# A decoder trunk in fp32: the two chunks behind each norm on unnormed tokens, and a reordered opening and last norm

## The reference, cut to what matters

```python
def rmsnorm(x, g):
    y = x * lax.rsqrt(jnp.mean(x * x, axis=-1, keepdims=True) + EPS)
    return y * g

c_act = jax.nn.silu(c)
for layer in range(2):
    shift, scale, gate = jnp.split(c_act @ ada_w[layer, 0] + ada_b[layer, 0], 3, axis=-1)
    hn = rmsnorm(x, norm_g[layer, 0]) * (1.0 + scale) + shift
    y = rglru_mlstm_mixer(hn, ...) if layer == 0 else stick_breaking_mixer(hn, ...)
    x = x + gate * y
    shift, scale, gate = jnp.split(c_act @ ada_w[layer, 1] + ada_b[layer, 1], 3, axis=-1)
    hn = rmsnorm(x, norm_g[layer, 1]) * (1.0 + scale) + shift
    x = x + gate * ((silu(hn @ w1) * (hn @ w3)) @ w2)
return rmsnorm(x, final_g)
```

## Time and profile before

| | |
|---|---|
| median of 3 runs | 2367.89 us (2367.54 to 2368.1) |
| profiled execution | 2365.77 us, its span 2363.9 us |
| PE busy | 2302.2 us (97%) |
| PEld, DVE, ACT, POOL busy | 1971.4, 1771.0, 940.4, 183.2 us |
| chain that ended last | PE 91%, DMA 4%, DVE 2%, issue 1%, ACT 1% |
| DMA | 619.80 MB, mean 262 GB/s |

### The profile page before, as it was taken

The page is one execution under the profiler, slowest core; times in us unless marked ns, Lnnn a source line. Parts: engine busy times, 40 slices in busy tenths (PEclk is TensorE's granted clock), DMA queues, the critical chain, the costliest instruction groups (busy, mean ns, idle before and its releaser), DMA issues.

```text
span 2363.9 us, 35433 instructions
## 1 busy us (share of the span) xinstructions
PE 2302.2 (97%) x12570; PEld 1971.4 (83%) x12570; DVE 1771.0 (75%) x2216; ACT 940.4 (40%) x1101; POOL 183.2 (8%) x177
## 2 busy tenths in 40 slices
PE   5999999999999999999999999998999999999998
PEld 3668888788888888888878888887888888888887
DVE  6766789888878888888976656599887566656665
ACT  2011343544433443344455554435443344433442
POOL 0000005200000000000500000260000000000012
PEclk9999999999999999999999999999999999999999
DMA  9998778577777777777866666576775555555554
GB/s 381 422 409 358 292 291 311 189 302 272 294 286 268 287 284 280 281 288 283 315 230 239 265 248 231 189 291 221 291 288 220 189 193 180 194 186 189 187 205 159
DMA packets 86616, 619.80 MB, mean 262 GB/s; under 512 B 10264, under 2 KB 10520, under 8 KB 11544
## 3 DMA queue, kind: packets, MB, share of 16 engines
q1 hardware_dynamic: 85680, 617.79, 68.7%
q10 hardware_dynamic: 872, 1.15, 0.1%
HBM read 616.80 MB, written 2.10 MB: 262 GB/s over the span
## 4 chain that ended last, share of the span: by engine, by line
PE 91%; DMA 4%; DVE 2%; issue 1%; ACT 1%; SPq 0%; POOL 0%; DVEq 0%; POOLq 0%; ACTq 0%
PE ps L1125 49%; PE ps L1123 12%; PE ps L1128 12%; PE ps L1075 6%; DMA adaw<-ada_dram 4%; PE ps L1062 3%; PE ps L1039 2%; DVE adaw L686 1%; PE ps L1086 1%; PE ps L1041 1%; PE ps L1092 1%; DVE wlow L678 1%; PE ps L1270 0%; PE ps L1170 0%; PE ps L1266 0%
## 5 line engine op out<-in xcount | busy, mean ns | idle before, releaser
L497 ACT ACTIVATE whigh<-raw 128x1024 fp32r<-128x1024 f32 x704 | 732.6, 1043 | 1024.1 <-PE ps L1125 996.1
L678 DVE TENSOR_TENSOR wlow<-raw,whigh 128x1024 fp32r<-128x1024 f32 x704 | 855.4, 1219 | 282.0 <-ACT whigh L497 268.9
L1125 PE MATMUL ps<-hn,whigh 128*128 128x512 f32 x3232 | 1018.1, 396 | 0.0
L1125 PE MATMUL ps<-mid,whigh 128*128 128x512 f32 x1856 | 585.1, 396 | 1.4 <-DVE wlow L678 0.8
L1125 PEld LDWEIGHTS ps<-hn,whigh 128*128 128x128 f32 x3232 | 493.2, 189 | 0.3
L1123 PE MATMUL ps<-hn,wlow 128*128 128x256 f32 x1616 | 449.7, 278 | 0.0
L1128 PE MATMUL ps<-hn,wlow 128*128 128x256 f32 x1616 | 448.2, 277 | 0.0
L686 DVE CUSTOM_DVE_ANT_0 adaw<-adaw,cact 128x2048 f32<-128x2048 f32 x152 | 354.2, 2332 | 28.5 <-DMA adaw<-ada_dram 28.5
L1123 PEld LDWEIGHTS ps<-hn,wlow 128*128 128x128 f32 x1616 | 303.3, 188 | 73.9
L1128 PEld LDWEIGHTS ps<-hn,wlow 128*128 128x128 f32 x1616 | 303.8, 188 | 69.2
L1125 PEld LDWEIGHTS ps<-mid,whigh 128*128 128x128 f32 x1856 | 283.3, 189 | 2.7 <-issue 2.0
(11 more groups left out here) (213 smaller groups left out, 1480.5 us busy)
## 6 DMA issues: line engine op xcount, KB each, us to landing
raw<-wts_dram SPq DMA_DIRECT2D x386, 1024.0 KB, 4.8
adaw<-ada_dram SPq DMA_DIRECT2D x152, 1024.0 KB, 6.7
adaw_more<-ada_dram SPq DMA_DIRECT2D x24, 1024.0 KB, 9.8
raw<-ada_dram SPq DMA_DIRECT2D x16, 1024.0 KB, 12.1
work<-wts_dram SPq DMA_DIRECT2D x6, 1024.0 KB, 10.4
x<-xT_dram SPq DMA_DIRECT2D x4, 512.0 KB, 11.1
out_dram<-x SPq DMA_DIRECT2D x4, 512.0 KB, 2.6
cact<-c_row_dram SPq DMA_DIRECT2D x1, 1024.0 KB, 4.8
```

The lines of the kernel that those rows point to most:

```text
L497: act.activation(whigh[:, (2 * s + h) % 4, 0:width], raw[:, s, h * HALF:h * HALF + width], ACT.Copy)\
L678: dve.tensor_tensor(wlow[:, half, 0:width], raw[:, s, h * HALF:h * HALF + width], whigh[:, half, 0:width].bitcast(F32), ALU.subtract).then ...
L1125: ins = pe.matmul(ps[:, s, :], whigh[:, half, w], src[:, kk, :, :], start=kk == 0, stop=kk == kts - 1, skip_group_check=True)
```

## The change

Four things are changed.

**Raw first chunks.** In the first body behind norms 1, 2 and 3, chunks 0 and 1 are no longer split. ScalarE makes `tokens`, x times slope without the root of the variance, one tile at a time during the last body before the norm (the last tile within the norm), and puts the shift beside it as a 257th column. TensorE multiplies the float32 chunk with these 257 columns (`raw_pair`), chunk 0 and then chunk 1, and runs the norm's own small products inside chunk 0, behind its tiles 6 and 10. VectorE multiplies the finished chunk by the kept 1/root and adds the column of the shift. Tile 15 is squared by ScalarE. The normed tokens are still made, for chunks 2 and 3 and the bodies behind, now in four scalings of four tiles and 16 low parts. Chunks 0 and 1 lie in places 2 and 3 of `raw`, and chunks 2 and 3 in places 0 and 1, where they are split in the body before.

**Banks and units.** Chunks of `k` are summed in banks 2, 3, 0, 1. The first `k` body takes four units in place of two, and the last `out1` body none in place of two.

**Softplus** is computed for both pairs of heads function by function. `fresh_half` asks for three split halves at its start and for the fourth at tile 8.

**Opening and last norm.** The reciprocal is taken at tile 0, before the units of tile 1, and the mixer's constants at tile 8. TensorE runs 56 small products before its first sum of squares and 14 behind it. The quarters of squares are added in another way. In the last norm ScalarE squares tile 15, the table for the root is loaded earlier, and TensorE runs three small products ahead of the sums and one behind them.

```diff
-RSTD_STEP = 1
-CONST_STEP = 3
+CONST_STEP = 8
+TOKEN_TILES = [(range(0, 3), range(3, 6)), (range(6, 9), range(9, 12)), (range(12, 13), ()), (range(13, 15), ())]
+VARIANCE_AT, SPREAD_AT = 6, 10
...
-    body(IN1 + 1, "k", 0, 0, 73, 2)
+    body(IN1 + 1, "k", 0, 0, 73, 4)
...
-    bodies(OUT1 + 1, DOWN - 1, "out1", 85, 2, i0=1)
+    bodies(OUT1 + 1, DOWN - 2, "out1", 86, 2, i0=1)
+    body(OUT1 + DOWN - 1, "out1", 0, DOWN - 1, 0, 0, last=True)
...
+def bank(kind, s):
+    return (s + 2) % CH if kind == "k" else s
...
+def split_next(n, s, raw_start_next):
+    if raw_start_next and s >= 2:
+        return n + 1, s, True
+    return (*split_lead(n, s), False)
...
+def place_of(s, raw_start):
+    return (s + 2) % CH if raw_start else s
...
+                        if starts_raw(kind, fresh) and held < 2:
+                            sp.wait_ge(S["halves_multiplied"], n * 8 + 2 * held + 2 + CREDIT)
+                        else:
+                            sp.wait_ge(S["low_ready"], n * 8 + 2 * held + 2)
...
+            def tokens_tile(norm, m):
+                if m >= 12:
+                    act.wait_ge(S["chunks_evicted"], LAST_UPDATE[norm] * CH + m + 1 + CREDIT)
+                act.activation(tokens[:, m, 0:T], x[:, m, :], ACT.Copy, scale=slope[:, m:m + 1]).then_inc(S["tokens_ready"], 1)
...
             def norm(i):
-                act.wait_ge(S["consts_ready"], 5)
-                act.activation(warm[:, :], epsb[:, :], ACT.Sqrt)
+                act.wait_ge(S["chunks_evicted"], LAST_UPDATE[i] * CH + KT + CREDIT)
+                act.activation(last_square, x[:, KT - 1, :], ACT.Square).then_inc(S["last_squared"], 1)
...
+            def rescaled(i, dst, s):
+                dve.tensor_copy(raw_col[:, s:s + 1], ps[:, s, T:T + 1]).then_inc(S["raw_columns"], 1)
+                dve.tensor_tensor(dst, ps[:, s, 0:T], rstd_kept, ALU.mult).then_inc(S["raw_scaled"], 1)
+
+            def scaled(i, j):
+                dve.wait_ge(S["tokens_ready"], (KT + 1) * (i - 1) + 4 * j + 5)
+                if j > 1:
+                    dve.wait_ge(S["hn_ready"], KT * (i - 1) + 4 * j - 4)
+                dve.tensor_tensor(normed(j), tokens[:, 4 * j:4 * j + 4, 0:T],
+                                  rstd_kept.rearrange("p (a t) -> p a t", a=1).to_broadcast([P, 4, T]), ALU.mult)\
                    .then_inc(S["scaled_ready"], 1)
...
-                pe.wait_ge(S["low_ready"], n * 8 + 4)
+                pe.wait_ge(S["low_ready"], n * 8 + 3)
                 for kk in range(KT):
+                    if kk == HK:
+                        pe.wait_ge(S["low_ready"], n * 8 + 4)
...
+            def raw_pair(n, kind):
+                norm = NORM_OF[kind]
+                for s in range(2):
+                    pe.wait_ge(S["chunks_evicted"], n * CH + s + 1)
+                    place = place_of(s, True)
+                    pe.wait_ge(weight_loaded[place], weight_count(n, place))
+                    for k in range(KT):
+                        pe.wait_ge(S["tokens_ready"], (KT + 1) * (norm - 1) + k + 2)
+                        ins = pe.matmul(ps[:, s, 0:T + 1], raw[:, place, k * P:k * P + P], tokens[:, k, :], start=k == 0, stop=k == KT - 1,
+                                        skip_group_check=True)
+                        if s == 0 and k == VARIANCE_AT:
+                            variance(norm)
+                        elif s == 0 and k == SPREAD_AT:
+                            spread(norm)
+                    ins.then_inc(S["halves_multiplied"], 2)
...
+            def variance(c):
+                pe.wait_ge(S["square_step"], 31 * c)
+                column_sums(squares_sum, True)
+                pe.wait_ge(S["last_squared"], c)
+                column_sums(last_square, False).then_inc(S["variance_ready"], 1)
...
                     pe.wait_ge(S["consts_ready"], 5)
-                    pe.wait_ge(S["squares_added"], 3)
-                    for m in range(4):
-                        ins = pe.matmul(ps[:, 7, 0:T], ones[:, :], start_squares[:, m, :], start=m == 0, stop=m == 3)
+                    keep_busy(56)
+                    for i, m in enumerate((12, 13, 0, 1)):
+                        pe.wait_ge(S["squares_added"], 3 + i // 2)
+                        ins = pe.matmul(ps[:, 7, 0:T], ones[:, :], start_squares[:, m, :], start=i == 0, stop=i == 3)
                     ins.then_inc(S["variance_ready"], 1)
+                    keep_busy(14)
```

More of the change, by code:

```diff
@@ L142, in run_stream @@
     body(OUT0 + 2, "out0", 0, 2, 39, 2)
-    body(OUT0 + 3, "out0", 0, 3, 40, 0)
+    body(OUT0 + 3, "out0", 0, 3, 40, 0, last=True)
     between("norm", 1)
@@ L174, in second_width, with starts_raw, raw_start_next @@
     return HALF
[L177 to L187 removed]
+def place_of(s, raw_start):
+    return (s + 2) % CH if raw_start else s
+def starts_raw(kind, fresh):
+    return fresh and kind in NORM_OF
+def raw_start_next(units, last):
+    return last and units >= 0
 def bass_trunk(nc, xT, c_row, wts, ada, ada_b, norm_g, wgate, conv, lru_w, lru_b, lam, gate_b, mnorm_g, out):
@@ L372, in full_body, with body @@
                             load_unit(u + 2)
-            def body(n, kind, q, i, pair, units, fresh=False, inner={}):
+            def body(n, kind, q, i, pair, units, fresh=False, inner={}, last=False):
                 if kind in FULL:
```

264 lines of the change are left out of this document (165 added, 99 removed).

## The result

The changed kernel takes 2338.15 us (median of 4 runs, 2336.82 to 2338.48), the kernel before 2367.9 us (4 runs, 2367.54 to 2368.1): a ratio of 0.9876, 95% interval 0.9862 to 0.989, so 29.7 us or 1.2% faster. The forecast was 2341 in a range of 2335 to 2352. The profiled execution took 2336.82 us, its span is 2335.1 us, 28.8 us less than before; forecast were 27.1.

What follows compares the result with a forecast made beforehand. TensorE was taken as the bound, 91% of the chain of waits, with long pauses and low clock behind them. Terms 17.8+6.6+2.4+0.3 = 27.1 us took the profiled 2365.77 to 2338.7; with 2.1 for the median, about 2341, range 2335 to 2352.

Steps and rivals of the forecast that it cites:

- Norms (17.8 us): Norms 1 to 3: a raw pair of 15.6 us replaces stretches of 20.1, 21.8 and 22.7, gaining 17.8 us.
- VectorE behind the norm: VectorE's norm work of 13.2 us ends at 461.8, so TensorE does not pause; bad end 0.9 us at norms 1 and 3.
- `out1` (6.6): Start of `out1`: the 3.97 us pause and half of 5.30 us at low clock go, gaining 6.6 us.
- Banks of k and the four-unit body (0): Attention: new bank order and two more units in the first k body change nothing; up to 2 us if VectorE overflows.
- Opening (2.4): Opening: tile 0 starts near 25, done at 32 before the DMA queue runs dry; gain 2.4 us, bounds 0.5 to 3.
- `out0` (0): `out0` may start 1.2 us sooner, but its pair ends on the mixer's last part, which does not move: zero.
- rival B: From the softplus-and-wait run's expectation: all 1.3 us at `out0` come from the three-halves wait, giving 2360.0 us.
- Last norm (0.3): Last norm: ScalarE's square of about 0.4 us replaces GpSimd's 0.61, and small products run at full clock: 0.3 us.
- 1: Norms: VectorE falls behind, costing 3 us a norm, 9 in sum, giving 2350 us; chance 0.13.
- 2: Pauses of `out1` and the opening stay, 9 us less gain, giving 2350 us; chance 0.09.
- 3: Slower: float32 matmuls with 257 columns take twice 0.43 us, costing 41.7 us more, giving 2382 us; chance 0.04.
- Rival 4: More gain than counted, as VectorE's shorter wait for splits frees the following bodies: 2336 us; chance 0.06.

Runs made afterwards that it cites:

- e3: The kernel before, with TensorE's pauses at norms 1 to 3 filled by 19 matmuls that nobody reads: 2364.01 us, ratio 0.9989.
- e6: The changed kernel with the spread of the reciprocal root behind tile 6 of the second raw chunk instead of tile 10 of the first: 2345.6 us, ratio 0.9913.
- e1: The kernel before with only the softplus table by table and the fresh pairs of out0 and out1 waiting for three halves, not four: 2359.94 us, ratio 0.9973.
- e10: The kernel before with the pauses of norms 1 to 3 filled by matmuls and VectorE's 16 scalings at each left out: 2356.7 us, ratio 0.9956.
- e7: The changed kernel without the 56 and 14 small products that keep TensorE busy in the opening: 2336.96 us, ratio 0.9877.
- e5: The changed kernel with the spread of the reciprocal root behind tile 15 of the first raw chunk instead of tile 10: 2338.2 us, ratio 0.9882.
- e2: The kernel before with only the softplus of the scores done table by table: 2363.05 us, ratio 0.9986.

## Why the prediction was right

**Norms (17.8 us).** 19.9 measured, 19.4 less what the bodies behind take back. The steps on which the sum rests were right: no pause ahead of the pair, PEclk 1.00, the root in time, 0.434 us per raw matmul. The mis-sized term is the new stretch: I set 15.6 us, it is 14.9, since the sums took 0.81 instead of 1.0, the spread 0.44 instead of 0.7, and chunk 2 starts before the end of the last raw matmul. That is 0.7 us three times. The sum took the old stretch as one number. Beside it stood a wrong reading, that the low clock costs 2.6 us of it at norm 1: e3 brought the clock back and the pair still took 13.38 us instead of 13.65, because VectorE paced it. The reading did not enter the sum, and so did no harm. At norm 1 the closeness is also luck, since the old stretch there lay anywhere from 19.0 to 21.3 us and the prediction had one profile of it.

**VectorE behind the norm.** I put its end at 461.8 against an old start of 442.1, 19.7 us behind; it was 456.61-439.02 = 17.6. Upper values for 21 operations in a row added up to 1.8 us of false load: the last seven low parts took 2.86 us, 0.41 each, not 0.48. My bad end of 0.9 us a norm never came; by e6 the margin is 2.5 us.

**`out1` (6.6).** 6.5 measured, and e1 with only these two edits gives the same 6.5. The working also named the right reason for needing three halves only. Of the 6.6, the 2.65 for the clock are the lucky part: behind the same pause of 3.97 us e3 and e10 paid 1.5 and 1.3. The masks cost no wait.
By the Trainium skill, SBUF — State Buffer, section Who interferes with whom, the port is held for a whole instruction and the loser is blocked. Eight masks at the quiet rate of the earlier trace rows are 2.06 us; they took 3.98, so 1.9 us were lost beside the two splits of VectorE, which ran for 2.59. That agrees roughly with the rule. My 0.5 us came from using it wrongly, with one split lost for each mask where there were only two splits.

**Banks of k and the four-unit body (0).** The attention stretch from chunk 2 behind norm 2 to `out1`, less the pause, is 288.83 us before, 288.78 in e1 without these edits, 288.84 after. Zero.

**Opening (2.4).** 1.8 against the profile of before, 3 and more against the other old openings. One step failed here: tile 0 near 25, with the squares in at 19.5 and the sums at full clock. The squares were in at 20.60, and behind the pause of 3.55 us ahead of them the clock was low, which I had allowed for only in the lower bound. It did not matter, because the other step held: what counts is the stream, and tile 0 was done at 35.24, early enough for it (36.27 in e7 was, too). My range of 0.5 to 3 was made from one profile of an opening that differs by 2.9 us between profiles, so that 2.4 came near is partly luck.

**`out0` (0).** -1.3 in the pair of profiles. I had said that its pair ends on the last part of the mixer. In fact TensorE, before, waited 1.21 us ahead of the pair for the fourth half and 0.56 in chunk 2. From the first full chunk to chunk 2, five kernels without the new wait need 219.7 to 220.6 us, nine with it 218.7 to 220.7, on average 0.6 less; the wait for three halves may be the cause, and the rest of the 1.3 looks like scatter. e1's median, 2359.94, is at rival B's 2360.0 and not at 2360.8, but its interval is wider than that difference. I count this as not settled.

**Last norm (0.3).** The second pair of sums waited 0.54 us for ScalarE's square, and the spread came 2.70 us behind the last matmul instead of 2.95: 0.25 us, as forecast. The span did not end sooner for it, 13.20 us behind that matmul instead of 13.07; this end piece lay between 13.07 and 13.61 us in all kernels, so a gain of 0.3 can't be seen.

```profile
2323.44 0.61 PE L1277 MATMUL ps<-ones,work 128*128 128x1 f32 x4 [0.54 <-ACT work L625]
```

**Rivals.** 1 fell with e5, 2 with the rows of `out1` and the 422 GB/s of the opening, 3 with 0.434 us for a matmul of 257 columns against the 0.432 of the earlier trace rows. Rival 4, more gain than counted, is the side on which the forecast missed, by 1.7 us of span, though not through freed bodies behind the norms: these took 0.5 back, for a reason that stays open. The median missed by 2.8 us, and the other 1.1 are mostly the step from profile to median: I took 2.1 us from one pair of numbers, and here it was 1.3.

## What to carry to other kernels

Ask of a slow stretch what would still hold it if the first cause went: at the norms the clock and VectorE hid each other, and only e10, which took both away, brought the pair to its full speed. Ask also what the new code costs against the old stretch as it really ran: dearer arithmetic was free here. Before timing an edit to the opening of a kernel, look whether a later point (here the last units of a full DMA stream) starts at the same time in all versions; if so, little ahead of it is worth work. And where, as in `fresh_half`, the last of several buffers comes free only with the consumer's own last instruction, a wait for all of them has a floor that no faster producer removes (2.56 us in e2); ask for fewer.
